# Two experts of the second layer loaded before the expert loop: the loop's block count is worked out from two items further on

## The chip, the cores and the metric

One core of a Trainium2 chip runs the whole program. The metric is the device time of one execution in microseconds (us), and the figure compared is the median over runs. TensorE is called PE, VectorE DVE, ScalarE ACT and GpSimd POOL; SP is the engine whose queue issues nearly all loads.

## What is computed

Two transformer layers over 256 latent tokens and 256 context tokens, width 1024, all in float32. The second layer returns the latents only, so its expert stage handles 256 tokens. What matters here is that stage:

```python
def moe(h, prm):
    t = h.reshape(B * N, D)
    scores = jax.nn.sigmoid((t @ prm["w_router"]).astype(jnp.float32))
    _, idx = lax.top_k(scores + prm["b_router"].astype(jnp.float32), TOP_K)      # 4 of 32 experts
    sel = jnp.take_along_axis(scores, idx, axis=-1)
    w = sel / jnp.sum(sel, axis=-1, keepdims=True) * ROUTED_SCALE
    ...
    gate = jnp.einsum("td,edf->tef", t, prm["w_gate_e"])      # 1024 x 256 for each expert
    up = jnp.einsum("td,edf->tef", t, prm["w_up_e"])          # 1024 x 256
    act = jax.nn.silu(gate) * up * comb[..., None]
    routed = jnp.einsum("tef,efd->td", act, prm["w_down_e"])  # 256 x 1024
```

Ahead of it in each layer stand the latents and attention (MLA), a short convolution, a Fourier mixing, 24 sigmoid gate groups that merge the three, and one output projection (`w_out`, 1024 x 1024).

## The kernel before

**Items.** The expert stage works in items. An item is one expert with up to `CAP[l]` of its tokens: 128 in the first layer, 64 in the second. Items 0 to 31 are experts 0 to 31. An expert with more tokens than `CAP[l]` gets a further item, and these follow as items 32, 33 and so on. DVE counts how many items hold tokens (`turns[0, 1]`, L2051 and after) and compares the count with `item_t[:, 4:8]`, which holds 32, 36, 40 and 44. The number of these four values that lie below the count is `more`.

**The loop.** Four items (`UNROLL`, u = 0 to 3) make a block. Block 0 stands ahead of the loop, written out; SP, POOL, ACT, PE and DVE then each run `Fori(1, more + BLOCKS)` with `BLOCKS` = 8. So 4 x (8 + `more`) items are run. An item behind the last one with tokens still loads weights (those of expert 0) and is computed; its column in the table of rows is the "absent" one, so it gathers and stores no row.

**An item's work.** SP loads 3 MiB of weights: gate and up, 1 MiB each, into `ring[u]` (`load_gate_up`, L656) and down, 1 MiB, into `dn[u]` (`load_down`, L671). A load into buffer u waits until PE has read the buffer for the item four earlier (`gu_full`, `y_full`). SP issues in order, so a load that waits holds back those behind it. POOL gathers the item's token rows from DRAM (L826) and stores its result rows (L838), half a row of 512 floats (2 KiB) to a partition in the second layer. PE transposes the rows (L1521), multiplies by gate and up (L1547: 8 chunks of the depth x 2 column halves, 256 columns each), transposes the activation (L1556) and multiplies by down (L1572). ACT and DVE take the results from PSUM.

**Ahead of the loop in the second layer.** SP walks through `stream`, a list in which each entry names its buffer (`slot`), who must have read the buffer before, and the source. `ukv` sits in slot 3, `uq` in slot 0, branch weights in the halves "0" and "0b", gate weights in slots 1 and 2 (slot 2 lies in `qkv`), and the two halves of `w_out` in slots 1 and 3, both loaded after the gates of the last branch. Then come gate/up of item 0 and down of items 0 and 1 (wait: last `y` group), after the output projection `tri`, the shared expert's weights into `ring[3]` (2 MiB), gate/up of items 1 and 2, down of items 2 and 3, and, once the shared expert has been multiplied (`sgu 1 1`), gate/up of item 3. The loop follows.

**The output projection.** For each half j of `w_out` and each of 8 chunks k, ACT makes a rounded copy (L1058) and DVE the remainder (L1951); PE (L1435 to L1437) multiplies with both, half j after half.

Of the kernel before, what the change touches and what calls it, by code (L numbers as in the profile page):

```python
# [16 lines left out]
P = 128  # L17
KC = DM // P
# [13 lines left out]
ROUNDS = 4  # L32
ADA_CHUNKS = 12
MAX_ITEMS = 48
# [145 lines left out]
def hybrid_layers(nc, I, C, out):  # L180
# [23 lines left out]
    with ctx:  # L204
# [64 lines left out]
        needed, over = part(1), part(4)  # L269
# [19 lines left out]
        h_hi = ring_lo[:, 2, :].rearrange("p (k t) -> p k t", k=KC)  # L289
# [23 lines left out]
        mT = qkv[:, 0:4096].rearrange("p (k t) -> p k t", k=KC)  # L313
# [10 lines left out]
        id_of = qkv[:, 688:704].rearrange("p (t k) -> p t k", k=TOPK)  # L324
        row_of_item = m_lo[:, 4:8, :].rearrange("p a b -> p (a b)").rearrange("p (n c) -> p n c", c=P)
# [15 lines left out]
        item_col, item_expert = tab[0:1, 136:136 + MAX_ITEMS], tab[0:1, 184:184 + MAX_ITEMS]  # L341
# [11 lines left out]
        gu = [ring[:, u, :].rearrange("p (a k n) -> p a k n", a=2, k=KC) for u in range(UNROLL)]  # L353
        gu_lo = [ring_lo[:, u, :].rearrange("p (a k n) -> p a k n", a=2, k=KC) for u in range(UNROLL)]
# [63 lines left out]
        gu_full = by_layer("gu_full")  # L418
        gu_part, e_hi_ready, e_lo_ready = one("gu_part"), one("e_hi_ready"), one("e_lo_ready")
# [58 lines left out]
        for l in range(DEPTH):  # L478
# [76 lines left out]
            for j, n in ((0, "1"), (1, "3")):  # L555
                item(n, ("psum", (l, "out", last, 1)), (l, "out", j), KC, at(I["w_out"][l], 512 * j, 512 * j + 512))
# [51 lines left out]
        def out_weights(l, j, k):  # L608

            n = stream[item_at[(l, "out", j)]][4]  # L610
            flat = lambda w: w[:, :, :, :].rearrange("p a k n -> p (a k n)")[:, 512 * (k % 4):512 * (k % 4) + 512]
            high = h_lo[:, k, :] if j else flat(w_hi if k < 4 else w_lo)
            return slot(l, "out", j)[:, k, :], high, area_lo[n][:, 512 * k:512 * k + 512]
# [14 lines left out]

        block = ctx.enter_context(nc.Block())

        @block.sync
        def _(sp):
# [15 lines left out]
            for l in range(DEPTH):  # L648
                act = ACTIVE[l]
                for n in range(first_item[l] + (3 if l else 0), first_item[l + 1]):  # L650
# [20 lines left out]
                def load_down(u, b, e, first=False):  # L671
                    if not first:
                        sp.wait_ge(y_full[l], 4 * b + u - 3)
# [6 lines left out]


                load_gate_up(0, 0, 0, first=True)
                for u in (0, 1):
                    load_down(u, 0, u, first=True)
# [4 lines left out]
                w = ring[:, SLOTS - 1, :].rearrange("p (a n) -> p a n", a=2)  # L689
                sp.dma_start(w[:, 0, :], by_p(I["w_gate_s"][l])).then_inc(shared_loaded, 16)  # L690
                sp.dma_start(w[:, 1, :], by_p(I["w_up_s"][l])).then_inc(shared_loaded, 16)
                load_gate_up(1, 0, 1, first=True)
                load_gate_up(2, 0, 2, first=True)
                for u in (2, 3):
                    load_down(u, 0, u, first=True)
                load_gate_up(3, 0, 3, first=True)
                wait_emptied(sp, l, "items")
                more = sp.value_load(more_u[0:1, 0:1], min_val=0, max_val=4)
                with nc.sync.Fori(1, more + BLOCKS) as b:
                    for u in range(UNROLL):  # L700
                        e = sp.value_load(item_expert[:, bass.ds(4 * b + u, 1)], min_val=0, max_val=NE - 1)
# [4 lines left out]
                if l == 0:  # L706
                    for n in range(first_item[1], first_item[1] + 3):
                        load_item(n)
                for u in range(UNROLL):
                    sp.wait_ge(y_stored[l][u], more * 16 + 16 * BLOCKS)  # L710
# [10 lines left out]
        def _(pool):  # L721
# [18 lines left out]
            for l in range(DEPTH):  # L740
# [34 lines left out]
                else:  # L775
                    pool.wait_ge(grow_stored, 48)
                    for n in range(2):
                        pool.dma_start(Grow[:, n, 0, :], grow_d[1][n:n + 1, :].to_broadcast([P, DM])).then_inc(grow_loaded, 16)

                for b in (1, 2):  # L780
                    for dc in range(KC):
                        n = (b - 1) * KC + dc
                        if l == 0 and n == 14:
                            load_cols(1)
                            pool.wait_ge(grow_stored, 32)
                            for s in range(2):
                                for m in range(2):
                                    pool.dma_start(Grow[:, m, s, :], grow_d[0][2 * s + m:2 * s + m + 1, :].to_broadcast([P, DM]))\
# [4 lines left out]
                        nc.gpsimd.tensor_tensor(mT[:, dc, 0:P * act], mT[:, dc, 0:P * act],  # L793
# [13 lines left out]

                def column(u, b):
                    return pool.value_load(item_col[:, bass.ds(4 * b + u, 1)], min_val=0, max_val=P)
# [7 lines left out]
                def gather(u, b, first=False):  # L817

                    n = u if first else column(u, b)
                    if not first:  # L820
                        pool.wait_ge(xt_full[l], 4 * b + u - 3)
# [3 lines left out]
                    copied((16 * b + 4 * u - 7) if not first else 2 * u + 1)  # L825
# [4 lines left out]
                def store(u, b, copies):  # L830

                    n = column(u, b)
                    pool.wait_ge(y_act[l], 4 * b + u + 1)
                    if l == 0:
# [5 lines left out]
                                            bounds_check=n_y, oob_is_err=False).then_inc(y_stored[l][u], 16)  # L840


                for u in range(UNROLL):
                    gather(u, 0, first=True)
                with nc.gpsimd.Fori(1, more + BLOCKS) as b:
                    for u in range(UNROLL):
                        gather(u, b)
                        store(u, b - 1, 16 * b + 4 * u - 5)
                for u in range(UNROLL):
                    store(u, more + (BLOCKS - 1), more * (4 * UNROLL) + (4 * NE - 7 + 2 * u))  # L850

        @block.scalar
        def _(act_e):
# [20 lines left out]
            for l in range(DEPTH):  # L874
# [49 lines left out]
                for k in range(KC):  # L924
                    nc.scalar.activation(h_hi[:, k, 0:n_tok], hT[:, k, 0:n_tok], ACT.Copy).then_inc(h_hi_ready[l], 1)
# [125 lines left out]
                for j in range(2):  # L1051
                    wait_arrived(act_e, l, "out", j)
                    for k in range(KC):
                        if j == 0:
                            act_e.wait_ge(merged[l], KC + k + 1)
                            nc.scalar.activation(h_hi[:, k, 0:n_tok], mT[:, k, 0:n_tok], ACT.Copy).then_inc(h_hi_ready[l], 1)
# [49 lines left out]

                def take_x(u, b, n=None):

                    act_e.wait_ge(xt_full[l], 4 * b + u + 1)
                    if n is None or n >= 2:  # L1110
                        act_e.wait_ge(gu_full[l], 4 * b + u - 1)
# [5 lines left out]
                def silus(u, b, n=None):  # L1117
                    act_e.wait_ge(gu_full[l], 4 * b + u + 1)
                    if n is None or n >= 2:
                        act_e.wait_ge(a_ready[l], 4 * b + u - 1)  # L1120
# [3 lines left out]
                def take_y(u, b, n=None):  # L1124

                    act_e.wait_ge(y_full[l], 4 * b + u + 1)
                    if n is None or n >= 2:

                        act_e.wait_ge(y_stored[l][(u - 2) % 4], 16 * b + (16 if u >= 2 else 0))
# [19 lines left out]
                else:  # L1149
                    for n in range(UNROLL):  # L1150
                        take_x(n, 0, n)
                        if n >= 1:
                            silus(n - 1, 0, n - 1)
                        if n >= 2:
                            take_y(n - 2, 0, n - 2)
# [37 lines left out]
        def _(pe):  # L1193
# [21 lines left out]
            for l in range(DEPTH):  # L1215
# [85 lines left out]
                for i, (name, f) in enumerate(IN_TILES):  # L1301
                    dst = group(l, name, f)
                    pe.wait_ge(w_lo_ready[l], i + 1)
                    for k in range(KC):
# [3 lines left out]
                        nc.tensor.matmul(dst[:, 0:n_tok], hi, h_hi[:, k, 0:n_tok], start=k == 0, stop=False)  # L1308
                        nc.tensor.matmul(dst[:, 0:n_tok], hi, h_lo[:, k, 0:n_tok], start=False, stop=False)  # L1309
                        ins = nc.tensor.matmul(dst[:, 0:n_tok], lo, h_hi[:, k, 0:n_tok], start=False, stop=k == KC - 1)  # L1310
# [89 lines left out]
                for b in range(3):  # L1400
                    for dc in range(KC):
# [5 lines left out]
                        for k in range(KC):  # L1407
                            hi, lo = w_hi[:, n % 2, k, :], gate_lo(l, n)[:, k, :]
                            nc.tensor.matmul(dst[:, 0:n_tok], hi, h_hi[:, k, 0:n_tok], start=k == 0, stop=False)  # L1409
                            nc.tensor.matmul(dst[:, 0:n_tok], hi, h_lo[:, k, 0:n_tok], start=False, stop=False)  # L1410
                            ins = nc.tensor.matmul(dst[:, 0:n_tok], lo, h_hi[:, k, 0:n_tok], start=False, stop=k == KC - 1)  # L1411
# [13 lines left out]
                for t in range(act):  # L1425
                    for j in range(2):
                        dst = group(l, "out", t, j)
                        for k in range(KC):
# [5 lines left out]
                            hi, lo = h_hi[:, k, tile(t)], m_lo[:, k, tile(t)]  # L1434
# [25 lines left out]
                def shared_in(f, a):  # L1460
# [3 lines left out]
                    w = gu[SLOTS - 1]  # L1464
# [20 lines left out]
                for n in range(act * TOPK):  # L1485
                    pe.wait_ge(id_ready, NTILE * TOPK * l + n + 1)
                    ins = nc.tensor.matmul(dst[:, 0:P], id_of_item[:, n, :], row_of_item[:, n, :], start=n == 0, stop=n == act * TOPK - 1)
# [24 lines left out]
                narrow = CAP[l] < P  # L1512

                def transpose_x(u, b, n=None):
                    pe.wait_ge(x_gathered[l][u], 16 * b + 16)
                    if n is None or n >= 1:
                        pe.wait_ge(xt_act[l], 4 * b + u)
                        pe.wait_ge(xt_dve[l], 4 * b + u)
# [5 lines left out]
                def gate_up(u, b):  # L1524
# [14 lines left out]
                    pe.wait_ge(gu_loaded[l][u], 32 * b + 32)  # L1539
                    pe.wait_ge(xt_act[l], 4 * b + u + 1)  # L1540
                    pe.wait_ge(xt_dve[l], 4 * b + u + 1)
                    x = xT[u % 2]
                    for k in range(KC):
                        xk = x[:, P * (k % 4) + 64 * (k // 4):P * (k % 4) + 64 * (k // 4) + 64]
                        for f in range(2):
                            w = gu[u][:, :, k, P * f:P * f + P]
# [4 lines left out]
                def transpose_a(u, b, n=None):  # L1551
                    pe.wait_ge(a_ready[l], 4 * b + u + 1)
                    if n is None or n >= 1:
                        pe.wait_ge(at_ready[l], 4 * b + u)
# [4 lines left out]
                def down(u, b, n=None):  # L1559
                    pe.wait_ge(at_ready[l], 4 * b + u + 1)  # L1560
                    pe.wait_ge(dn_loaded[l][u], 16 * b + 16)
                    if n is None or n >= 1:
                        pe.wait_ge(y_act[l], 4 * b + u)
                        if not narrow:
                            pe.wait_ge(y_dve[l], 4 * b + u)
                    for f in range(2):
                        for c in range(2):
                            if not narrow:
                                ins = nc.tensor.matmul(ps[:, 3072 + 512 * c:3584 + 512 * c], aT_e[u % 2][:, tile(f)],  # L1569
                                                       dn[u][:, f, 512 * c:512 * c + 512], start=f == 0, stop=f == 1)  # L1570
                            else:
                                ins = nc.tensor.matmul(ps[64 * c:64 * c + 64, 3072:3584], aT_e[u % 2][:, 64 * f:64 * f + 64],  # L1572
                                                       dn[u][:, f, 512 * c:512 * c + 512], start=f == 0, stop=f == 1,
# [3 lines left out]
                for n in range(UNROLL):  # L1577
# [681 lines left out]
```

## Time and profile before

| | us |
|---|---|
| median of 3 runs | 1688.69 |
| the runs | 1687.06 to 1694.16 |
| the profiled execution | 1688.29 |
| its span, first to last instruction | 1686.4 |

| | PE | DVE | ACT | POOL |
|---|---|---|---|---|
| busy, share of the span | 91% | 55% | 36% | 21% |

The profiled execution's time is 1.9 us more than its span. PE at 91% is an average over stages; the chain that ended last gives PE 69% of the span, DMA 14% and DVE 11%, and the line of DMA that stands out in it is the load of `in_w_up_e` with 10%. The mean granted clock of PE is 0.963 of 2.4 GHz. The second layer's expert loop is the last long stage, from 1366 us to 1645 us.

### The profile page before, as it was taken

What the parts mean: (1) busy time and instruction counts of PE and PEld (TensorE: products, weight loads), DVE (VectorE), ACT (ScalarE), POOL (GpSimd) and SP (SyncE); (2) the same over time, 40 slices, a digit from 0 to 9 for tenths busy, and PEclk for the clock granted to TensorE, in tenths of its full rate; (3) what the DMA queues carried; (4) which work ended last, traced back from release to release, by engine and by line L of the source; (5) the groups of instructions that cost most, each with busy time, mean ns of one, the idle gap of its engine ahead of it and who ended that gap; (6) DMA issues with size and microseconds to landing.
All of it is one profiled execution on the core that took longest, in us unless ns stands there. A gap on an engine that the chain in (4) does not pass through costs nothing.

```text
span 1686.4 us, 22672 instructions
## 1 busy us (share of the span) xinstructions
PE 1526.3 (91%) x7546; PEld 1064.8 (63%) x7546; DVE 919.8 (55%) x1579; ACT 599.8 (36%) x1034; POOL 352.8 (21%) x495
## 2 busy tenths in 40 slices
PE   5999999999988988999999987999999898888876
PEld 3677566677756755767767645866799664444442
DVE  1576778777885464777777734446656521110112
ACT  2332234423323433655656514334455511111111
POOL 3000000001112002465556520000011024333320
PEclk8999999999999989999999999999999999998998
DMA  9743340255566063899999973302255679999993
GB/s 334 255 155 123 125 150 1 76 200 189 185 239 230 31 252 128 294 369 359 364 371 367 354 249 119 124 29 100 88 188 191 252 264 414 415 414 415 416 372 138
DMA packets 122998, 393.88 MB, mean 234 GB/s; under 512 B 15556, under 2 KB 20116, under 8 KB 103472
## 3 DMA queue, kind: packets, MB, share of 16 engines
q1 hardware_dynamic: 104128, 359.42, 56.5%
q0 software_dynamic: 17440, 30.31, 5.2%
q10 hardware_dynamic: 1360, 3.23, 0.5%
q8 instruction: 43, 0.70, 0.2%
q14 instruction: 27, 0.22, 0.0%
HBM read 389.65 MB, written 30.50 MB: 249 GB/s over the span
## 4 chain that ended last, share of the span: by engine, by line
PE 69%; DMA 14%; DVE 11%; issue 2%; SPq 2%; ACT 1%; POOL 0%; POOLq 0%; DVEq 0%; ACTq 0%
PE ps L1212 14%; DMA ring<-in_w_up_e 10%; PE ps L1569 6%; PE ps L1547 3%; PE ps L1409 3%; PE ps L1532 3%; PE ps L1534 3%; PE ps L1533 3%; PE ps L1410 3%; PE ps L1411 3%; PE ps L1380 2%; DVE Grow L1712 2%; PE ps L1308 2%; PE ps L1309 2%; PE ps L1310 2%
## 5 line engine op out<-in xcount | busy, mean ns | idle before, releaser
L1547 PE MATMUL ps<-ring,oT_b 128*64 128x256 f32 x1152 | 154.2, 428 | 44.8 <-DMA ring<-in_w_up_e 44.2
L2073 DVE TENSOR_TENSOR ring_lo<-ring,m_lo 128x1024 fp32r<-128x1024 f32 x128 | 156.1, 1223 | 13.4 <-ACT m_lo L1094 4.0
L1547 PEld LDWEIGHTS ps<-ring,oT_b 128*64 128x64 f32 x1152 | 93.7, 153 | 96.9 <-DMA ring<-in_w_up_e 39.3
L1094 ACT ACTIVATE m_lo<-ring 128x1024 fp32r<-128x1024 f32 x128 | 135.5, 1061 | 42.3 <-PE ps L1534 31.9
L1409 PE MATMUL ps<-ring_lo,w_hi 128*128 128x512 f32 (+1 forms) x384 | 131.8, 343 | 3.9 <-DVE ring_lo L1899 3.7
L1712 DVE SCALAR_TENSOR_TENSOR Grow<-ring,small,Grow 128x512 f32<-128x512 f32 x182 | 131.1, 749 | 3.8
L2105 DVE TENSOR_TENSOR head<-ps,head 128x128 f32<-128x128 f32 (+1 forms) x68 | 23.9, 351 | 197.5 <-ACT head L1121 197.5
L1410 PE MATMUL ps<-h_lo,w_hi 128*128 128x512 f32 (+1 forms) x384 | 130.1, 339 | 0.0
L793 POOL TENSOR_TENSOR qkv<-qkv,head 128x512 f32<-128x512 f32 (+1 forms) x32 | 36.1, 1127 | 432.4 <-DVE head L1931 432.4
L838 POOL DMA_INDIRECT y_rows<-bT,small x68 | 99.3, 1460 | 27.2 <-issue 27.2
L1532 PE MATMUL ps<-m_lo,oT_lo 128*128 128x512 f32 x256 | 103.3, 404 | 0.0
L1533 PE MATMUL ps<-ring_lo,oT_lo 128*128 128x512 f32 x256 | 100.5, 392 | 0.0
L1534 PE MATMUL ps<-m_lo,h_lo 128*128 128x512 f32 x256 | 100.5, 392 | 0.0
L836 POOL COPY small<-wr 128x1 uint32 x68 | 34.4, 506 | 279.3 <-ACT bT L1130 148.3
L1308 PE MATMUL ps<-ring_lo,oT_lo 128*128 128x512 f32 (+1 forms) x256 | 87.1, 340 | 5.1 <-DVE ring_lo L1756 5.0
L1121 ACT ACTIVATE head<-ps 128x128 f32<-128x128 f32 (+1 forms) x68 | 21.8, 320 | 194.1 <-PE ps L1547 189.1
L1409 PEld LDWEIGHTS ps<-ring_lo,w_hi 128*128 128x128 f32 x384 | 73.6, 192 | 23.0 <-issue 14.1
L1309 PE MATMUL ps<-h_lo,oT_lo 128*128 128x512 f32 (+1 forms) x256 | 86.0, 336 | 0.0
L1035 ACT ACTIVATE tmp<-ps,small 128x512 f32<-128x512 f32 (+1 forms) x48 | 28.0, 583 | 160.6 <-PE ps L1411 160.0
L1410 PEld LDWEIGHTS ps<-h_lo,w_hi 128*128 128x128 f32 x384 | 73.7, 192 | 7.2
L1310 PE MATMUL ps<-ring_lo 128*128 128x512 f32 (+1 forms) x224 | 77.0, 344 | 0.0
L1212 PE MATMUL ps<-ring,hT 128*128 128x288 f32 (+1 forms) x224 | 64.3, 449 | 4.4 <-DVE hT L1741 4.4
(324 smaller groups left out, 3317.1 us busy)
## 6 DMA issues: line engine op xcount, KB each, us to landing
ring<-in_w_gate_e SPq DMA_DIRECT2D x68, 1024.0 KB, 9.5
ring<-in_w_up_e SPq DMA_DIRECT2D x68, 1024.0 KB, 13.8
ring<-in_w_ada SPq DMA_DIRECT2D x34, 1024.0 KB, 5.4
qkv<-in_w_down_e SPq DMA_DIRECT2D x34, 1024.0 KB, 14.6
ring<-in_w_in SPq DMA_DIRECT2D x13, 2048.0 KB, 10.1
cT<-in_w_down_e SPq DMA_DIRECT2D x17, 1024.0 KB, 9.4
fT<-in_w_down_e SPq DMA_DIRECT2D x17, 1024.0 KB, 11.0
qkv<-in_w_in SPq DMA_DIRECT2D x7, 2048.0 KB, 11.4
```

Of the source, the lines that this page charges most:

```text
L1094: nc.scalar.activation(pair(e_hi, j), pair(gu[u], j), ACT.Copy).then_inc(e_hi_ready, 1)
L1212: ins = nc.tensor.matmul(dst, a, b, start=n == 0, stop=n == len(pairs) - 1)
L1308: nc.tensor.matmul(dst[:, 0:n_tok], hi, h_hi[:, k, 0:n_tok], start=k == 0, stop=False)
L1309: nc.tensor.matmul(dst[:, 0:n_tok], hi, h_lo[:, k, 0:n_tok], start=False, stop=False)
L1409: nc.tensor.matmul(dst[:, 0:n_tok], hi, h_hi[:, k, 0:n_tok], start=k == 0, stop=False)
L1410: nc.tensor.matmul(dst[:, 0:n_tok], hi, h_lo[:, k, 0:n_tok], start=False, stop=False)
L1532: nc.tensor.matmul(ps[:, o:o + 512], hi, e_hi[:, :, k, :], start=k == 0, stop=False)
L1533: nc.tensor.matmul(ps[:, o:o + 512], hi, gu_lo[u][:, :, k, :], start=False, stop=False)
L1534: ins = nc.tensor.matmul(ps[:, o:o + 512], lo, e_hi[:, :, k, :], start=False, stop=k == KC - 1)
L1547: ins = nc.tensor.matmul(ps[64 * f:64 * f + 64, o:o + 256], xk, w, start=k == 0, stop=k == KC - 1, skip_group_check=True)
L1712: ins = V.scalar_tensor_tensor(into, w[:, k, :], by, into, ALU.mult, ALU.add)
L2073: V.tensor_tensor(pair(gu_lo[u], j), pair(gu[u], j), pair(e_hi, j).bitcast(f32), ALU.subtract).then_inc(e_lo_ready, 1)
```

## The change

In the second layer two experts are handled ahead of the four-item blocks (`AHEAD = [0, 2]`). Their 6 MiB of weights are loaded early into places that the second layer leaves half used, since it has 256 tokens where the first has 512:

- expert 0: gate and up into `ring[3]`, down into the context half of `xres`, issued behind `uq` and waiting for the last `kvup` group; behind it expert 1's gate into half of `ring[2]` and its up into half of `Grow`
- expert 1's down into half of the old `mT` area, issued behind the second gate item

Buffer u of block b now holds item 4b + u + 2. The written-out part has six items: two in buffers u = 2, 3 (block -1) and four of block 0. Item 1's gate and up lie apart, so PE multiplies them in two groups of 128 columns where all others take one of 256. The four thresholds for `more` become 34, 38, 42 and 46. The shared expert goes into `ring[1]`. Before the loop, gate/up of item 2 is loaded after the output projection, that of item 3 after the shared expert, that of item 5 after item 0's gate/up multiply and that of item 4 after item 1's. The second half of `w_out` goes into slot 0 in two halves, the later of them waiting for the last `y` group. The rest makes room: `mT`, `m_lo`, `h_hi`, the table of rows and the gate rows are packed closer in the second layer.

```diff
+AHEAD = [0, 2]
-MAX_ITEMS = 48
+MAX_ITEMS = 52
...
+        ahead_gate = ring[:, 2, 2048:4096].rearrange("p (k n) -> p k n", k=KC)
+        ahead_up = early_acc[:, 2048:4096].rearrange("p (k n) -> p k n", k=KC)
+        ahead_dn = [w.rearrange("p (k n) -> p k n", k=2) for w in
+                    (xres[:, 2:4, :].rearrange("p t d -> p (t d)"), qkv[:, 2048:4096])]
...
-            for j, n in ((0, "1"), (1, "3")):
-                item(n, ("psum", (l, "out", last, 1)), (l, "out", j), KC, at(I["w_out"][l], 512 * j, 512 * j + 512))
+            out_read = ("psum", (l, "out", last, 1))
+            item("1", out_read, (l, "out", 0), KC, at(I["w_out"][l], 0, 512))
+            if l == 0:
+                item("3", out_read, (l, "out", 1), KC, at(I["w_out"][l], 512, 1024))
+            else:
+                for i in range(2):
+                    item(("0", "0b")[i], out_read, (l, "out", 1, i), 4, at(I["w_out"][l][512 * i:512 * i + 512], 512, 1024), half=True)
...
+        prologue = lambda l: [(u, -1) for u in range(UNROLL - AHEAD[l], UNROLL)] + [(u, 0) for u in range(UNROLL)]
...
+                def load_ahead(i):
+
+                    by_k = lambda w: w[1, i].rearrange("(p k) n -> p k n", k=KC)
+                    if i == 0:
+                        wait_full(sp, 1, "kvup", NTILE - 1, 1)
+                    into = (gu[3][:, 0, :, :], gu[3][:, 1, :, :]) if i == 0 else (ahead_gate, ahead_up)
+                    sp.dma_start(into[0], by_k(I["w_gate_e"])).then_inc(ahead_loaded[i], 16)
+                    sp.dma_start(into[1], by_k(I["w_up_e"])).then_inc(ahead_loaded[i], 16)
...
+                    if l and stream[n][0] == (l, "uq"):
+                        load_ahead(0)
+                        load_ahead_down(0)
+                        load_ahead(1)
+                    if l and stream[n][0] == (l, "gate", 0, 1):
+                        load_ahead_down(1)
...
-                        sp.wait_ge(gu_full[l], 4 * b + u - 3)
+                        sp.wait_ge(gu_full[l], 4 * b + (u - 3 + off))
+                    elif l:
+                        if u == 1:
+                            wait_full(sp, l, "sgu", 1, 1)
+                        elif u >= 2:
+                            sp.wait_ge(gu_full[l], 4 - u)
...
+                    load_gate_up(0, 0, 2, first=True)
+                    for u in (2, 3):
+                        load_down(u, 0, u + off, first=True)
+                    load_gate_up(1, 0, 3, first=True)
+                    load_gate_up(3, 0, 5, first=True)
+                    load_gate_up(2, 0, 4, first=True)
...
+                    if early == 1:
+                        for a, w in enumerate((ahead_gate, ahead_up)):
+                            for k in range(KC):
+                                xk = x[:, P * (k % 4) + 64 * (k // 4):P * (k % 4) + 64 * (k // 4) + 64]
+                                for f in range(2):
+                                    ins = nc.tensor.matmul(ps[64 * f:64 * f + 64, o + P * a:o + P * a + P], xk, w[:, k, P * f:P * f + P],
+                                                           start=k == 0, stop=k == KC - 1, skip_group_check=True)
...
-                for n in range(UNROLL):
-                    transpose_x(n, 0, n)
+                seq = prologue(l)
+                for n in range(len(seq)):
+                    transpose_x(*seq[n], n)
...
-                link(V.tensor_scalar(over[0:1, :], item_t[0:1, 4:8], turns[0:1, 1:2], None, ALU.is_lt))
+                link(V.tensor_scalar(over[0:1, :], item_t[0:1, 4:8], float(AHEAD[l]), turns[0:1, 1:2], ALU.add, ALU.is_lt))
```

## Rows read from the trace of the kernel before

**Rows 1.** Windows in layer 2: us, busy us (instructions), PEclk, DMA share, GB/s

```profile
1102.00:1140.00 38.00, 36.28 (x173) 24.69 (x173) 12.47 (x24) 10.98 (x26) 0.00 (x0) 1.00 0.09 32
1140.00:1196.00 56.00, 52.11 (x255) 34.41 (x254) 39.34 (x104) 24.45 (x56) 0.00 (x0) 1.00 0.20 75
1196.00:1217.00 21.00, 19.13 (x147) 19.08 (x147) 11.52 (x18) 10.53 (x17) 0.00 (x0) 0.92 0.29 101
...
1373.00:1379.40 6.40, 6.28 (x47) 3.39 (x47) 1.27 (x4) 0.94 (x3) 0.00 (x0) 1.00 0.89 328
...
1391.00:1417.00 26.00, 25.27 (x187) 14.34 (x185) 3.72 (x13) 5.42 (x14) 12.01 (x25) 1.00 1.02 414
1417.00:1645.00 228.00, 184.18 (x1212) 102.05 (x1211) 24.89 (x82) 32.53 (x82) 74.46 (x159) 0.91 1.00 406
```

**Rows 2.** Waits from 1366 us to 1660 us: who for whom, us, times, longest

```profile
PE ps L1547 <- DMA ring<-in_w_up_e: 44.2, 28, 2.9
```

**Rows 3.** SP's queue in order of time: start us, us, line, what is loaded

```profile
1303.79 0.34 SPq L668 DMA_DIRECT2D ring<-in_w_gate_e  x1
...
1366.27 0.34 SPq L668 DMA_DIRECT2D ring<-in_w_gate_e  x1
...
1373.20 0.35 SPq L668 DMA_DIRECT2D ring<-in_w_gate_e  x1
...
1380.73 0.34 SPq L668 DMA_DIRECT2D ring<-in_w_gate_e  x1
```

**Rows 4.** Issue to landing of the up loads issued at 1373.66 and 1622.14

```profile
DMA to landing us min/median/max: 8.9/8.9/8.9
...
DMA to landing us min/median/max: 23.1/23.1/23.1
```

**Rows 5.** The last two stores of result rows, in POOL's timeline

```profile
1654.46 1.01 POOL L838 DMA_INDIRECT y_rows<-bT,small  x1 [0.54 <-issue]
...
1657.35 1.00 POOL L838 DMA_INDIRECT y_rows<-bT,small  x1 [0.80 <-issue]
```

**Rows 6.** POOL's DMA queue, windows 1654.5:1657.3 and 1657.3:1659.6: packets, MB, share

```profile
q0 software_dynamic: 80, 0.02, 3.1%
...
q0 software_dynamic: 80, 0.00, 1.7%
```

**Rows 7.** The chain that ended last, its last stage: start us, us, what

```profile
1374.04 3.60 PE ps L1547 x32
1377.64 1.72 PE ps L1572 x8
...
1613.28 0.23 issue
...
1622.14 23.06 DMA ring<-in_w_up_e
1645.19 0.23 issue
1645.42 5.36 PE ps L1547 x32
```

**Rows 8.** PE's weight loads of one item's gate and up, in the timeline

```profile
1369.33 3.22 PEld L1547 LDWEIGHTS ps<-ring,oT_b 128*64 128x64 f32 x32 [0.17 <-issue]
```

**Rows 9.** PE's timeline: the `kvup` groups, and the first gate group

```profile
1118.05 13.97 PE L1212 MATMUL ps<-ring,qkv 128*128 128x512 f32 x32 [0.94 <-ACT oT_b L956]
...
1197.95 0.36 PE L1409 MATMUL ps<-ring_lo,w_hi 128*128 128x256 f32 x1 [1.87 <-DVE ring_lo L1899]
```

**Rows 10.** Splitting `w_out` in ACT's and DVE's timeline, second half last

```profile
1309.35 4.27 ACT L1058 ACTIVATE h_lo<-ring 128x512 fp32r<-128x512 f32 x8
...
1312.17 4.89 DVE L1951 TENSOR_TENSOR ring_lo<-ring,h_lo 128x512 fp32r<-128x512 f32 x8
```

**Rows 11.** Issue to landing of gate at 1303.79 and the second down load

```profile
DMA to landing us min/median/max: 4.8/4.8/4.8
...
DMA to landing us min/median/max: 11.0/11.0/11.0
```

More of the change, by code:

```diff
@@ L268, in hybrid_layers @@
         sel = item_t[:, 8:10]
-        needed, over = part(1), part(4)
+        needed = part(1)
         half_id = part(1)
@@ L418, in hybrid_layers @@
         gu_full = by_layer("gu_full")
+        ahead_loaded = [one(f"ahead_loaded_{i}") for i in range(2)]
+        ahead_stored = [one(f"ahead_stored_{i}") for i in range(2)]
         gu_part, e_hi_ready, e_lo_ready = one("gu_part"), one("e_hi_ready"), one("e_lo_ready")
@@ L708, in _ @@
                         load_item(n)
+                all_stored = more * 16 + 16 * BLOCKS
                 for u in range(UNROLL):
-                    sp.wait_ge(y_stored[l][u], more * 16 + 16 * BLOCKS)
+                    sp.wait_ge(y_stored[l][u], all_stored)
+                for i in range(off):
+                    sp.wait_ge(ahead_stored[i], 16)
                 for t in range(act):
@@ L828, in gather, with store @@
                                             bounds_check=n_g, oob_is_err=False).then_inc(x_gathered[l][u], 16)
-                def store(u, b, copies):
-                    n = column(u, b)
-                    pool.wait_ge(y_act[l], 4 * b + u + 1)
+                def store(u, b, copies, first=None):
+                    n = column(u, b) if first is None else first
+                    pool.wait_ge(y_act[l], 4 * b + (u + 1 + off))
                     if l == 0:
@@ L839, in store @@
                                             in_=y_e[u % 2][:, 0:wide[l]], in_offset=None,
-                                            bounds_check=n_y, oob_is_err=False).then_inc(y_stored[l][u], 16)
-                for u in range(UNROLL):
-                    gather(u, 0, first=True)
+                                            bounds_check=n_y, oob_is_err=False)\
+                        .then_inc(ahead_stored[first] if l and first is not None and first < off else y_stored[l][u], 16)
+                seq = prologue(l)
+                for n, (u, b) in enumerate(seq):
+                    gather(u, b, first=n)
+                    if n >= UNROLL:
+                        store(*seq[n - UNROLL], 16 * b + (4 * u - 5 + 4 * off), first=n - UNROLL)
                 with nc.gpsimd.Fori(1, more + BLOCKS) as b:
@@ L847, in _ @@
                         gather(u, b)
-                        store(u, b - 1, 16 * b + 4 * u - 5)
+                        store(u, b - 1, 16 * b + (4 * u - 5 + 4 * off))
                 for u in range(UNROLL):
-                    store(u, more + (BLOCKS - 1), more * (4 * UNROLL) + (4 * NE - 7 + 2 * u))
+                    store(u, more + (BLOCKS - 1), more * (4 * UNROLL) + (4 * NE - 7 + 2 * u + 4 * off))
         @block.scalar
@@ L1600, in _ @@
                     if t == act - 1:
-                        pe.wait_ge(y_act[l], more * UNROLL + NE)
+                        pe.wait_ge(y_act[l], more * UNROLL + (NE + off))
                         if not narrow:
```

201 lines of the change are left out of this document (119 added, 82 removed).

## The prediction

> **What bounds the kernel now.** I read the shares of busy time first and trusted them least: PE at 91% is an average. Then the windows of the second layer [rows 1]. Up to 1217 us DMA is nearly idle (share 0.09, 0.20, 0.29). From 1391 to 1417 us it is full at 414 GB/s, and from 1417 to 1645 us full at 406 GB/s, while DVE and ACT work a tenth of the time. The waits say the same: in the expert loop PE waited for the up load 28 times, 44.2 us in all [rows 2]. The chain of waits closes it: for each block of four items it goes once through "DMA ring<-in_w_up_e", 23.06 us for the last one, then PE [rows 7]. So from about 1373 us on the time is set by how many MiB are still to be moved, and by nothing that an engine does.
>
> One load checks this. The up load of item 4 is issued at 1373.66 and lands 8.9 later, at 1382.6; that of item 35, issued at 1622.14, lands 23.1 later, at 1645.2 [rows 4]. Between them lie 31 items of 3 MiB, so 93 MiB in 262.6 us, 2.82 us for a MiB with the rows that POOL gathers and stores in between. Bare, a MiB (1.049 MB) at 414 GB/s takes 2.53 us. The last block, whose items hold few rows, took from 1613.28 to 1645.19, 31.9 us for 12 MiB, 2.66 us each [rows 7].
>
> **How many items will run.** This is the step on which all hangs. The change saves only if `more` becomes 0, which needs at most 34 items with tokens. The profile of before tells how many there are. Item 34, the 35th, is stored by the second to last store, issued at 1654.46, and item 35 by the last, issued at 1657.35 [rows 5]. POOL's DMA queue moved 0.02 MB for the former and 0.00 MB for the latter, with as many packets [rows 6]. An absent row moves nothing, and a token's result is two halves of 2 KiB, so 0.02 MB are about five tokens. The 35th item holds tokens, the 36th none: `turns` is 35. Before, 35 lies above 32 and not above 36: `more` is 1 and 36 items run. After, 35 lies above 34 and not above 38: `more` is again 1, and 2 + 4 x 9 = 38 items run, not 34. Items 35, 36 and 37 are empty and load 3 MiB each all the same.
>
> **The sum, in MiB.** Count what is still to be loaded once the shared expert is done, at 1366.27 [rows 3]. Before: 36 x 3 less gate/up of items 0 to 2 (6) and four down loads (4), so 98. After: 38 x 3 less the 6 ahead, gate/up of item 2 (2) and four down loads (4), so 102. Two experts came out of the loop's traffic, two empty ones went in, and one ring buffer less is filled beforehand, since `ring[1]` holds the shared expert, `ring[3]` expert 0 and half of `ring[2]` expert 1. The difference is +4 MiB. Bounds: 4 x 2.53 = 10.1 us if they carry no rows at all, 4 x 2.82 = 11.3 us at the loop's mean. I take the last block's 2.66, since the added items are empty like most of that block: +10.6 us.
>
> The Trainium skill (DMA: Bandwidth & Descriptors, Specifications) gives a limit of about 358 GB/s for one core's reads from HBM. The rows do not bear it out here, at 414 GB/s. By that rule, as an estimate, the 4 MiB would cost 11.7 us.
>
> **The start of the loop, where DMA could fall idle.** Before, SP issues item 3's gate/up at 1366.27, item 4's at 1373.20 when item 0's multiply ends, item 5's at 1380.73 [rows 3]. After, the same two places carry items 3 and 5; item 4's follows item 1's multiply, which ends at 1374.04 + 3.60 = 1377.6 [rows 7], earlier than the 1380.73 of before. Item 6's follows item 2's multiply, about 6 us later, while DMA is still busy with item 4's. Before left DMA about 0.1 idle from 1373 to 1379.4 [rows 1], under 1 us. So the new order costs nothing, or gives back up to 0.7.
>
> Against it stands item 1's multiply in groups of 128 columns: as many columns, twice as many weight loads. Not in the trace; the bounds are 0 (the columns' 3.60 us stays) and +3.6 (32 loads show 3.22 us busy [rows 8], and 64 would take 6.4 and more). All later issues slip by it, and DMA has about 2 us of queued work against that. I take 0 of cost, with 1.6 at the worst end.
>
> The Trainium skill (TensorE: Matmul & The Clock Gate, Back-to-back issue gap) says that a stream of pairs of weight load and 128-column matmul sustains some 81 ns each, where one alone takes 56. As an estimate, 64 of them are 5.2 us, 1.6 more than the row's 3.60. That would stay under the 2 us, so the sum would not move; no row here shows it.
>
> **What is hidden, and by what.** The first 5 MiB ahead wait for the last `kvup` group, which is multiplied from 1118.05 and done at about 1132 [rows 9]. At 414 GB/s they take 12.7 us, to about 1147. Behind them in SP's queue stand the first branch and gate weights, which PE needs only with the first gate group at 1197.95 [rows 9]: over 40 us of cover. The sixth MiB goes at 1196 behind a gate load, with DMA at 0.29 [rows 1]; 2.5 us. Without that cover each MiB would cost 2.5 us. These loads also take nothing off the path before 1366: DMA is not what the router and the shared expert wait for.
>
> The later half of `w_out`'s second half now waits for the last `y` group, so it goes where item 0's gate load went, at 1303.79 [rows 3], and that one landed in 4.8 us, at 1308.6 [rows 11]. ACT begins that half of `w_out` at 1309.35 and spends 4.27 on 8 chunks, so the fifth comes at 1311.5; DVE starts at 1312.17 [rows 10]. 2.9 us of slack, cost 0. At the other end, if it shares the engines with the two down loads behind it and lands as late as the second of those (11.0 [rows 11], 1314.8), ACT stalls for 3.3 us, and PE with it. Added waits at the end of SP's program (`ahead_stored`) are met long before. POOL's written-out part is as long as before with its stores 4 behind. The rest is renaming. From the last up landing at 1645.2 to the end of the span 41 us stay as they are, but for PE's clock: item 35's multiply took 5.36 us where others took 3.60 [rows 7], after a wait in a stretch whose granted clock is 0.91 on the mean [rows 1]; this can fall the other way by 1.7.
>
> **Sum.** 1688.3 (the profiled execution) + 10.6 = 1698.9 us. The median of before, 1688.69, stands 0.4 from it. That is +0.6%.
>
> **Rivals.**
> - *It does as it says: 34 items.* It decides at whether the 35th item holds tokens. Then 34 x 3 - 12 = 90 MiB remain instead of 98, and 8 MiB less are 8 x 2.66 = 21.2 us: 1667. For it: only the stated number. Against it: the 0.02 MB of item 34's store [rows 6]. Chance 0.06.
> - *38 items, but the extra is partly given back.* Bare rate (10.1), the 0.7 of idle DMA gone, the last multiply as fast as the others (1.7): +7.7, 1696.0, inside 0.5%. Chance 0.22.
> - *38 items and the covers fail.* `w_out` lands late (+3.3) and item 1's multiply at double time idles DMA (+1.6): +15.5, 1703.8. Chance 0.12.
> - *Forecast*: 0.60, about 1697 to 1702.
>
> Some 0.5% (8.4 us) is what a measurement can tell from no change. The forecast and the third rival lie above it: slower 0.72. The second rival: same 0.21. The first, and a remainder of other gains: faster 0.07. The range of 8 in 10 takes the forecast, most of the second rival and the lower edge of the third, 1694.5 to 1704.
>
> **What would show it.** 38 gate loads, 38 stores and a last store with 0.00 MB in the second layer; three of the last four items without rows. Up loads from the one landing near 1382.6 to the last: 97 MiB in about 273 us. The first loads ahead at about 1132, DMA share up in that window and no new wait of PE before 1300. ACT's fifth chunk of `w_out` without a wait. The end of the span 41 us behind the last up landing. Wrong would be: 34 stores in the second layer, a loop shorter by 21 us, or a stall of PE in the output projection.

## The result

The changed kernel takes 1701.1 us (median of 4 runs, 1699.6 to 1703.0), the kernel before, beside it, 1689.6 us (1687.1 to 1694.2). The ratio is 1.0062, with an interval of 95% from 1.0045 to 1.0079: slower by 10.5 us, 7.6 to 13.3. (The two medians lie 11.5 us apart; the ratio is estimated from all the runs and not from the medians. For the experiments below the distance of the medians is given beside the ratio.) The forecast was 1698.9 in a range of 1694.5 to 1704. A second comparison on other runs gave 1.0063 (1.0045 to 1.0081), with medians of 1702.1 and 1690.7. All these runs are fast ones. 38 items ran, not 34.

The page of the profile after: the span, then the busy shares, then SP's DMA queue (packets, MB, share).

```profile
span 1699.6 us, 22982 instructions
...
PE 1538.9 (91%) x7668; PEld 1072.7 (63%) x7668; DVE 922.1 (54%) x1585; ACT 602.9 (35%) x1040; POOL 358.5 (21%) x507
...
q1 hardware_dynamic: 105264, 365.71, 56.9%
```

Busy shares tell nothing: PE is at 91% in both. The bytes of SP's queue do: 365.71 MB. The same line of before:

```profile
q1 hardware_dynamic: 104128, 359.42, 56.5%
```

That is 6.3 MB or 6 MiB more, just two more items of 3 MiB.

### The profile page after: what moved, and what is told of

It reads as the page before. It is cut to its first block, busy times and chain, and to the rows that moved or that the text cites. A ratio compares the mean times of both kernels' runs of the same rounds, so it can differ in the third digit from the quotient of the medians.

```text
span 1699.6 us, 22982 instructions
## 1 busy us (share of the span) xinstructions
PE 1538.9 (91%) x7668; PEld 1072.7 (63%) x7668; DVE 922.1 (54%) x1585; ACT 602.9 (35%) x1040; POOL 358.5 (21%) x507
## 3 DMA queue, kind: packets, MB, share of 16 engines
q1 hardware_dynamic: 105264, 365.71, 56.9%
## 4 chain that ended last, share of the span: by engine, by line
PE 71%; DMA 14%; DVE 10%; issue 2%; SPq 2%; ACT 1%; POOL 0%; DVEq 0%; POOLq 0%; ACTq 0%
PE ps L1287 14%; DMA ring<-in_w_up_e 10%; PE ps L1663 6%; PE ps L1635 4%; PE ps L1608 3%; PE ps L1610 3%; PE ps L1609 3%; PE ps L1484 3%; PE ps L1486 3%; PE ps L1485 3%; PE ps L1455 2%; DVE Grow L1807 2%; PE ps L1383 2%; PE ps L1597 2%; PE ps L1384 2%
## 5 line engine op out<-in xcount | busy, mean ns | idle before, releaser
L1635 PE MATMUL ps<-ring,oT_b 128*64 128x256 f32 x1184 | 157.9, 427 | 43.9 <-DMA ring<-in_w_up_e 43.9
L1163 ACT ACTIVATE m_lo<-ring 128x1024 fp32r<-128x1024 f32 x128 | 135.5, 1061 | 42.2 <-PE ps L1610 31.9
L901 POOL COPY small<-wr 128x1 uint32 (+1 forms) x70 | 34.7, 496 | 281.1 <-ACT bT L1204 150.9
L1184 ACT ACTIVATE oT_lo<-ps 128x1024 fp32r<-128x1024 f32 x32 | 32.8, 1026 | 98.7 <-issue 69.0
## 6 DMA issues: line engine op xcount, KB each, us to landing
qkv<-in_w_down_e SPq DMA_DIRECT2D x35, 1024.0 KB, 10.4
ring<-in_w_in SPq DMA_DIRECT2D x13, 2048.0 KB, 10.1
```

The costliest lines, as they stand in the source:

```text
L1163: nc.scalar.activation(pair(e_hi, j), pair(gu[u], j), ACT.Copy).then_inc(e_hi_ready, 1)
L1635: ins = nc.tensor.matmul(ps[64 * f:64 * f + 64, o:o + 256], xk, w, start=k == 0, stop=k == KC - 1, skip_group_check=True)
```

## The profile after, beside the rows of before

**How many items ran.** The DMA issues in the window of the second layer's expert stage, first of the kernel before, then of the changed one (the count behind x is that of the stores, one for each item):

```profile
y_rows<-bT,small POOLq DMA_INDIRECT x36, 6.6
```

```profile
y_rows<-bT,small POOLq DMA_INDIRECT x38, 6.6
```

POOL's timeline of the changed kernel, its last four stores, items 34 to 37:

```profile
1654.05 1.03 POOL L903 DMA_INDIRECT y_rows<-bT,small  x1 [0.55 <-issue]
1659.94 1.02 POOL L903 DMA_INDIRECT y_rows<-bT,small  x1 [0.51 <-issue]
1668.08 1.01 POOL L903 DMA_INDIRECT y_rows<-bT,small  x1 [0.42 <-issue]
1671.13 1.01 POOL L903 DMA_INDIRECT y_rows<-bT,small  x1 [0.85 <-issue]
```

And POOL's DMA queue in the window behind each of them (packets, MB, share), in the same order:

```profile
q0 software_dynamic: 79, 0.02, 1.5%
...
q0 software_dynamic: 80, 0.00, 0.6%
...
q0 software_dynamic: 80, 0.00, 1.3%
...
q0 software_dynamic: 80, 0.00, 1.7%
```

Item 34 carries 0.02 MB, as before [rows 6]; items 35, 36 and 37 carry nothing. Each of the three still had 3 MiB of weights loaded for it.

**The loop.** The chain of waits of the changed kernel, its last stage:

```profile
1372.27 5.31 PE ps L1635 x32
...
1378.60 3.64 PE ps L1627 x64
1382.24 1.72 PE ps L1666 x8
...
1629.01 0.23 issue
...
1637.65 22.96 DMA ring<-in_w_up_e
1660.61 0.23 issue
1660.84 3.67 PE ps L1635 x32
```

It has the shape of before [rows 7]: through the up load once a block, and 31.6 us from 1629.01 to 1660.61 for the last block, where before took 31.9. The last landing has moved from 1645.2 to 1660.6, 15.4 us. The span grew by 13.2. To split that, take SP's queue of the changed kernel:

```profile
1105.56 0.39 SPq L671 DMA_DIRECT2D ring<-in_w_uq  x1
1134.98 0.34 SPq L683 DMA_DIRECT2D ring<-in_w_gate_e  x1
...
1306.72 0.37 SPq L671 DMA_DIRECT2D ring<-in_w_out  x1
...
1369.05 0.34 SPq L719 DMA_DIRECT2D ring<-in_w_gate_e  x1
...
1377.60 0.33 SPq L719 DMA_DIRECT2D ring<-in_w_gate_e  x1
...
1382.28 0.33 SPq L719 DMA_DIRECT2D ring<-in_w_gate_e  x1
```

The kernel before issues `uq` at

```profile
1102.62 0.39 SPq L646 DMA_DIRECT2D ring<-in_w_uq  x1
```

- Up to `uq`, ahead of anything that the change alters in the order of the loads, the changed kernel is already 2.9 us late. From `uq` to the first load after the shared expert it takes 263.5 us, before 263.7 [rows 3]. The 2.9 us lie ahead of `uq` and vary: over nine profiles (those of the experiments below included) `uq` goes out between 1102.6 and 1111.7. Three profiles of the old structure have 1102.6, 1104.9 and 1108.2, mean 1105.2; six of the new one have 1105.6 to 1111.7, mean 1107.8. With that scatter an offset of the change ahead of `uq` is neither shown nor excluded.
- From that load to the last up landing: 291.6 us where before took 278.9, +12.6 (1369.05 to 1660.61, and 1366.27 to 1645.19).
- From the last landing to the end: 39.0 us where before took 41.2, -2.2. Of these 1.7 are item 35's 5.36 us, now 3.67 for item 37; the rest are the last read of result rows and the last multiply of the span, 0.4 and 0.4, with small steps against them.

The windows of the last item's gate/up multiply, before and after, in the columns of [rows 1]. The third number from the end is PE's granted clock as a share of 2.4 GHz:

```profile
1645.40:1650.80 5.40, 5.38 (x34) 3.98 (x36) 0.00 (x0) 0.00 (x0) 0.38 (x1) 0.68 0.18 71
...
1660.80:1664.50 3.70, 3.66 (x34) 2.98 (x36) 0.00 (x0) 0.00 (x0) 0.17 (x1) 1.00 0.19 73
```

The same multiply ran at a mean of 0.68, between 1.2 and 2.4 GHz, before, and at 2.4 GHz after. This repeats: 5.36 us in all three profiles of the old structure (and in that of three items ahead, below), 3.67 in all five of the structure with two items ahead.

**The start of the loop and the hidden parts.** Windows of the changed kernel: us, busy us (instructions) of PE, PEld, DVE, ACT and POOL, then PE's clock, DMA share, GB/s.

```profile
1102.00:1140.00 38.00, 36.09 (x185) 25.41 (x185) 14.51 (x28) 12.04 (x27) 0.00 (x0) 1.00 0.20 70
1140.00:1196.00 56.00, 52.11 (x249) 34.53 (x247) 39.34 (x104) 21.78 (x52) 0.00 (x0) 1.00 0.37 143
...
1352.00:1366.00 14.00, 12.72 (x62) 10.42 (x62) 7.80 (x31) 2.05 (x3) 1.85 (x5) 1.00 0.07 23
1366.00:1373.00 7.00, 5.03 (x29) 3.73 (x29) 1.27 (x3) 0.77 (x2) 4.82 (x10) 0.98 0.49 162
1373.00:1379.40 6.40, 6.28 (x49) 3.83 (x47) 0.98 (x3) 0.66 (x2) 0.53 (x1) 0.76 0.69 261
...
1417.00:1656.00 239.00, 197.47 (x1317) 109.60 (x1315) 26.50 (x87) 35.46 (x87) 80.88 (x171) 0.91 1.01 411
```

The early MiB show as DMA share 0.20 and 0.37 where before had 0.09 and 0.20 [rows 1], and PE is as busy as before in 1140 to 1196, 52.11 us. From 1373 to 1379.4 DMA stands at 0.69 where before had 0.89. Item 0's multiply took 5.31 us, at a granted clock of 0.68 from 1372.2 to 1377.6, and SP can issue item 5's load only behind it, at 1377.60, 8.6 us behind the one ahead of it. Before it, from 1369.0 to 1372.3, PE had stood idle for 1.36 and 0.61 us around a short group of transposes.

It looks as if 1.7 us of the +12.6 were the clock at this one place. The second profile of the same kernel says no. There the pauses are 1.27 and 0.60 us, the clock stays at 1.00, the multiply takes 3.63 and the distance is 6.8 us, and still the stretch from the first load to the last up landing is 291.9 us. The first 41 us of that stretch, in the kernel before, the changed one and its second profile:

```profile
1366.27:1407.27 41.00, 38.85 (x298) 22.22 (x300) 6.82 (x21) 7.51 (x19) 16.50 (x36) 1.00 0.95 366
...
1369.05:1410.05 41.00, 38.94 (x316) 23.09 (x318) 6.82 (x21) 7.64 (x19) 15.26 (x34) 0.96 0.89 346
...
1370.72:1411.72 41.00, 39.03 (x332) 23.52 (x334) 6.82 (x21) 7.63 (x19) 16.45 (x36) 1.00 0.94 357
```

At 406 GB/s the bytes missing against before are worth 2.0 us in the first profile and 0.9 in the second. In the rest of the stretch DMA moves 406 GB/s before and in the first profile, and 404 in the second, which is another 1.2 us. So a loss of about 2 us repeats, but not at one place, and its cause stays open.

**The output projection.** Waits of PE from 1303 to 1335, after:

```profile
PE ps L1510 <- DVE ring_lo L2046: 2.1, 1, 2.1
```

Before has the same single wait of 2.1 us there. ACT's second half of `w_out`, after:

```profile
1312.28 4.27 ACT L1127 ACTIVATE h_lo<-ring 128x512 fp32r<-128x512 f32 x8
```

Eight chunks in 4.27 us, exactly as before [rows 10]. The last quarter of `w_out`, issued at 1306.72, landed in 5.2 us, at 1311.9; ACT's fifth chunk comes at 1314.4, so it was there 2.5 us ahead.

## The experiments

The theory: the end is set by how many MiB are still to be moved once the shared expert is done, at 2.5 to 2.7 us each. The rival: empty items are nearly free, and the other parts of the change (split multiply, moved `w_out`, early loads, order of the first loads) cost the 10.5 us. Each run is given against the kernel before on the same chip.

**Fewer items by other data.** One expert's bias is lowered, so that 34 items hold tokens.

```diff
+                if l:
+                    link(V.tensor_scalar(biased[:, 0:act, 9:10], biased[:, 0:act, 9:10], -0.05, None, ALU.add))
                 for t in range(act):
                     link(V.max(m8[:, t, :], biased[:, t, :]))
```

> The changed kernel, with 0.05 taken off the router's bias of expert 9 in the second layer. That expert then has about 50 tokens instead of 76 and the items with tokens should fall from 35 to 34, so the block count drops by one; the output differs from the reference for the tokens that change expert. Theory A (the time goes by the MiB still to be moved after the shared expert): 90 MiB where the kernel before has 98, so 8 x 2.66 = 21 us less than before, about 1668 us, and 12 MiB or 32 us less than the changed kernel. Theory B (empty items are cheap, and the 11.5 us of the change come from its other parts: the split multiply, the moved half of w_out, the later start of the loop): at most a few us less than the changed kernel, 1695 us or more. 34 stores of result rows in the second layer under both.

Measured: 0.9874 (0.9853 to 0.9896), 1670.9 us against 1691.5. The stores of the stage:

```profile
y_rows<-bT,small POOLq DMA_INDIRECT x34, 6.4
```

That is 20.6 us less than before and, adding the two comparisons, 31 to 32 us less than the changed kernel. The same code but for the two added lines, with the count of items on the other side of a threshold, goes from slower to clearly faster. The rival's other parts are all still in it. At the price of the next two experiments, 2.48 and 2.52 us a MiB, the 8 MiB less come to 19.8 to 20.2 us, so those other parts together cost nothing that shows. Of the 8 MiB, 6 belong to the two items that do not run; only 2 are room gained, since 12 MiB are loaded before the shared expert is done where before had 10.

The same data on the kernel before, with the same two lines added:

> The kernel before with the same 0.05 taken off expert 9's bias; the output differs from the reference for the tokens that change expert. 34 is still above 32, so 36 items run, two of them empty. Theory A and B: within 1 us of the kernel before. Were it faster by several us, the rows moved and not the weights would set the loop's time, and the first run of this call would have to be read against this one.

Measured: 1.0009 (0.9994 to 1.0024), 1693.2 us against 1691.5. The medians lie 1.7 us apart, a little over the expected 1 us, but the interval includes no change. The data by themselves change nothing that can be measured.

**More items in the kernel before.**

```diff
-                link(V.tensor_scalar(over[0:1, :], item_t[0:1, 4:8], turns[0:1, 1:2], None, ALU.is_lt))
+                link(V.tensor_scalar(over[0:1, :], item_t[0:1, 4:8], -4.0 * l, turns[0:1, 1:2], ALU.add, ALU.is_lt))
```

> The kernel before with its thresholds in the second layer lowered by 4, so that one more block runs: 40 items, 5 of them empty. Theory A: 12 MiB more, 12 x 2.53 to 12 x 2.66 = 30 to 32 us more than before, about 1720 us. Theory B: an empty block costs what its multiplies cost at most, 4 x 6.0 = 24 us if PE set the pace, and near 0 if it is hidden.

Measured: 1.0176 (1.0154 to 1.0198), 1721.3 us, +29.7 for four empty items, 2.48 us a MiB and just under the 30 to 32 expected. Its waits for the up load, where before had 44.2 us in 28 waits [rows 2]:

```profile
PE ps L1547 <- DMA ring<-in_w_up_e: 51.0, 29, 2.8
```

An empty item costs 7.4 us. PE's instructions need 6.0 us for an item, as the start of the loop in the kernel before shows, where the multiplies follow each other without a wait for weights (1374.04, 1380.05 and 1386.08, by the chain of waits). So the item costs more than its computation; that the rest is its bytes is for the next experiment to show.

**Fewer bytes, the same items.** In the changed kernel's loop only half of each down load is made.

```diff
-                    sp.dma_start(dn[u], I["w_down_e"][l][bass.ds(e, 1)].rearrange("a (k p) n -> p (a k) n", p=P))\
-                        .then_inc(dn_loaded[l][u], 16)
+                    src = I["w_down_e"][l][bass.ds(e, 1)].rearrange("a (k p) n -> p (a k) n", p=P)
+                    if l and not first:
+                        sp.dma_start(dn[u][:, 0:1, :], src[:, 0:1, :]).then_inc(dn_loaded[l][u], 16)
+                    else:
+                        sp.dma_start(dn[u], src).then_inc(dn_loaded[l][u], 16)
```

> The changed kernel with the down loads inside the second layer's loop cut to the first of their two halves (the second half keeps the block before's weights; the output differs from the reference). The same 38 items and the same number of DMAs, 32 x 0.5 = 16 MiB less. Theory A (bytes): 16 x 2.53 to 16 x 2.66 = 40 to 43 us less than the changed kernel, unless PE's 6.0 us an item gets in the way, which it should not (38 items leave DMA at 7.0 us an item). A rival, that a fixed cost of an item or of a DMA sets the pace and not its bytes: under 5 us less.

Measured: 0.982 (0.98 to 0.9841), 1661.8 us, where the changed kernel beside it took 1702.1. 40.3 us less for 16 MiB, 2.52 us each. Same items, same count of DMAs: it is the bytes. A window in the middle of this kernel's loop:

```profile
1400.00:1600.00 200.00, 178.05 (x1311) 100.51 (x1309) 26.45 (x87) 35.59 (x87) 83.13 (x175) 0.99 1.02 411
```

DMA is still full at 411 GB/s, with PE close behind at 178 of 200 us.

**Is loading early worth anything?** The six MiB are issued after the output projection instead.

```diff
-                    if l and stream[n][0] == (l, "uq"):
-                        load_ahead(0)
-                        load_ahead_down(0)
-                        load_ahead(1)
-                    if l and stream[n][0] == (l, "gate", 0, 1):
-                        load_ahead_down(1)
...
+                if l:
+                    load_ahead(0)
+                    load_ahead_down(0)
+                    load_ahead(1)
+                    load_ahead_down(1)
                 if l == 0:
                     load_gate_up(1, 0, 1, first=True)
```

> The changed kernel with the six early MiB issued only after the output projection, behind the shared expert's weights, instead of during latents and gates. Theory A as in the prediction: what is loaded after the shared expert stays 102 MiB, but 6 MiB more have to pass between 1333 and 1366 us, where 7 MiB (shared 2, item 2's gate and up 2, two down loads 2, and 1 of token rows) passed before. DMA stood at 0.07 from 1352 to 1366, so 5 to 6 MiB fit there: 0 to 4 us more than the changed kernel. If each MiB loaded early were worth its 2.66 us, it would be 16 us more.

Measured: 1.0074 (1.0053 to 1.0095), 1704.0 us against 1702.1 for the changed kernel: +1.9, with runs that overlap (1701.2 to 1706.0 and 1698.9 to 1705.3). Its windows before the loop:

```profile
1352.00:1359.00 7.00, 6.35 (x33) 5.34 (x34) 6.55 (x26) 0.00 (x0) 0.00 (x0) 0.56 1.01 373
1359.00:1366.00 7.00, 7.00 (x40) 5.96 (x39) 3.94 (x19) 1.67 (x2) 0.00 (x0) 0.95 1.01 424
1366.00:1373.00 7.00, 6.79 (x32) 5.64 (x30) 0.27 (x2) 0.38 (x1) 4.09 (x9) 1.00 0.68 262
```

The loads fill the stretch that stood at 0.07 in the changed kernel. The last load behind them, the down load issued at about 1345, lands at 1371 to 1372, just ahead of the first load after the shared expert at 1372.82. From `uq` to that load this kernel takes 263.9 us, 0.4 more than the changed one, while the other kernels spread from 262.5 to 263.9. From there to the last up landing it takes 291.5 us, as in the changed kernel's profiles. What counts is that the MiB are in place when the loop begins. That they are loaded during attention brings about 2 us by the medians, and with runs that overlap that much nothing is shown.

**All 35 items and no more.** A third item stands ahead of the blocks, so that 3 + 32 = 35 run. Its weights go into `ring[0]` and the last down buffer after the output projection, and the blocks take the ring's parts in the order in which they fall free. The rest follows from `off = 3`.

```diff
-AHEAD = [0, 2]
+AHEAD = [0, 3]
...
+        gu_late = [gu[1], gu[3], gu[2], gu[0]]
...
-                    load_gate_up(0, 0, 2, first=True)
-                    for u in (2, 3):
-                        load_down(u, 0, u + off, first=True)
-                    load_gate_up(1, 0, 3, first=True)
-                    load_gate_up(3, 0, 5, first=True)
-                    load_gate_up(2, 0, 4, first=True)
+                    by_k = lambda w: w[1, 2].rearrange("(p k) n -> p k n", k=KC)
+                    sp.dma_start(gu[0][:, 0, :, :], by_k(I["w_gate_e"])).then_inc(ahead_loaded[2], 16)
+                    sp.dma_start(gu[0][:, 1, :, :], by_k(I["w_up_e"])).then_inc(ahead_loaded[2], 16)
+                    load_down(2, 0, 5, first=True)
+                    load_ahead_down(2)
+                    load_gate_up(0, 0, 3, first=True)
+                    load_gate_up(1, 0, 4, first=True)
+                    load_gate_up(2, 0, 5, first=True)
+                    load_gate_up(3, 0, 6, first=True)
+                    load_down(3, 0, 6, first=True)
```

> The changed kernel with three items ahead of the blocks instead of two, so that 3 + 4 x 8 = 35 items run, each of them with tokens. The third one's weights are not loaded early: gate and up go into ring[0] and down into the last down buffer after the output projection, as item 2's do now; the ring buffers of the blocks are taken in the order in which they come free. Theory A: 105 - 6 - 2 - 4 = 93 MiB after the shared expert where before has 98, 5 x 2.66 = 13 us less than before, about 1676 us. Theory B: no better than the changed kernel by more than 5 us, about 1696 us or more.

Measured: 0.9932 (0.9905 to 0.9959), 1680.4 us against 1691.5: faster than both kernels, by 11.2 us than the one before (13 were expected) and, adding the comparisons, some 22 us than the changed one.

```profile
y_rows<-bT,small POOLq DMA_INDIRECT x35, 6.9
```

**All of them on one line.** From SP's first load after the shared expert to the end of the span, which leaves out the first layer's scatter. The MiB are counted as in the prediction.

| kernel | items | MiB left | first load, us | span, us | between, us | to the last up landing | behind it |
|---|---|---|---|---|---|---|---|
| changed, half down loads | 38 | 86 | 1369.67 | 1661.9 | 292.2 | 252.8 | 39.5 |
| changed, other data | 34 | 90 | 1375.56 | 1674.9 | 299.3 | 259.7 | 39.6 |
| 3 ahead | 35 | 93 | 1370.53 | 1677.2 | 306.7 | 265.7 | 41.0 |
| before | 36 | 98 | 1366.27 | 1686.4 | 320.1 | 278.9 | 41.2 |
| before, other data | 36 | 98 | 1370.69 | 1690.7 | 320.0 | 279.1 | 41.0 |
| changed | 38 | 102 | 1369.05 | 1699.6 | 330.6 | 291.6 | 39.0 |
| changed, second profile | 38 | 102 | 1370.72 | 1703.3 | 332.6 | 291.9 | 40.6 |
| changed, loads late | 38 | 102 | 1372.82 | 1703.5 | 330.7 | 291.5 | 39.2 |
| before, one block more | 40 | 110 | 1368.39 | 1719.1 | 350.7 | 310.0 | 40.8 |

From 90 to 110 MiB it is 51.4 us for 20 MiB, 2.57 us each. No difference shows between 34 and 35 items with tokens, nor from when the early weights were loaded. What was not varied is the traffic of the token rows, which goes through POOL's queue, 8.1 to 8.2 MB in every profile of this stretch: 2.57 us is the price of a MiB of weights on top of it. The kernel with half down loads lies some 3 us above the line; PE is close behind DMA there.

The last two columns split the distance and show what the sum hides. Within one structure the price is even: 12 MiB cost 31.9 us from 90 to 102 in the changed kernel (2.66 each), and 31.0 from 98 to 110 in the old one (2.58 each). But from the old structure (98) to the changed one (102) the 4 MiB come with 12.4 to 13.0 us, about 2 more than at that price. Behind the last landing the changed kernel gives 0.3 to 2.2 us back, as its last multiply takes 3.67 us and not 5.36. The two differences oppose each other, and the column "between" lies on one line.

## Why the prediction was right

- **The bound and the count of items** were right. `turns` is 35, read from the 0.02 MB of one store. The profile after shows 38 items, three of them empty, and the run with 34 shows the other branch at -20.6 us, where the first rival said -21.2.
- **+4 MiB at 2.66 us** was right in mechanism and in price: 2.66 and 2.58 us within either structure, 2.48 and 2.52 by the medians of the experiments. (In its count the text speaks of one ring buffer less; the +4 MiB are two, as only item 2's gate and up go there ahead of time where before items 0 to 2 did. The sum is right.)
- **That the total came so close is in part luck.** The stretch to the last up landing grew by 12.4 to 13.0 us in three profiles against two, outside the sum's own bounds of 10.1 to 11.3; the tail shrank by 0.3 to 2.2 us. What was off by 2 us one way and by up to 2 us the other gave +10.4 to +12.6 us between the first load and the end.
- **The start of the loop "costs nothing, or gives back up to 0.7"** was not borne out. A loss of about 2 us repeats in all three profiles. The row of DMA at 0.69 shows part of it in the first one only, and no run shows its cause.
- **Item 1's split multiply at 0** was right: 64 records in 3.64 us, where an unsplit one takes 3.60, so 57 ns each. The Trainium skill's sustained 81 ns for pairs of weight load and 128-column matmul (TensorE: Matmul & The Clock Gate, Back-to-back issue gap) does not hold for these weights of 64 columns; the row is at the lone matmul's 56. The estimate of 1.6 us more did not come about.
- **`w_out` at 0** was right, without a new wait: 2.5 us of slack where 2.9 were worked out.
- **The limit of 358 GB/s** (the Trainium skill, DMA: Bandwidth & Descriptors, Specifications) is passed again: 411 GB/s over 239 us, with one core running the program.
- **"Without that cover each MiB would cost 2.5 us"** was wrong. The late loads had no such cover and cost 0.3 us each by the medians, and nothing by the distances within the profiles. I had seen only the first idle stretch of DMA as cover; the second one, 1352 to 1366, right ahead of the loop, takes 6 MiB as well. The cover itself was there: the first five loads ahead go out at 1134.98 and the last of them lands at about 1151. (1132 and 12.7 us give 1145 and not the 1147 of the text, and the loads took 16 us; against over 40 us neither matters.)
- **The tail** of 41 us came out at 39.0, 40.6 and 39.2. The 1.7 us of the last multiply's clock, which the second rival counted in, were gained each time; why PE is granted 2.4 GHz there after the change was not tested; what PE did before it differs, as told at the end. The rest is the last multiply of the span, 8.7 to 10.1 us long in the three profiles.

## What to carry to other kernels

Before crediting a change with work it removes, find the number that decides it in the trace: here a threshold on a count that depends on the data, read from the bytes of the last stores. Where a loop runs in blocks, a shift of its start must be matched to the count of items, or padding eats the gain: 3 ahead were faster, 2 ahead slower. In a stage bound by DMA, count the MiB left at its start; here loading ahead paid by the room that it found, and no more for being early. And when a forecast comes true, compare its terms too: here two of them were off and made up for each other.

## What was not expected of the hardware

- 6 MiB more between the output projection and the loop, with DMA full from 1338 to 1366 at 373 to 424 GB/s, left the router's and the shared expert's chain as it was: 263.9 us, where eight other profiles have 262.5 to 263.9.
- Code with the same first layer reaches `uq` at times 6 us apart from profile to profile (1102.6 to 1108.2 in the old structure, 1105.6 to 1111.7 in the new one), more than half of the effect looked for. Only distances within one profile could tell the parts apart.
- The same last multiply of an item was granted 0.68 of 2.4 GHz in each of the three profiles of the old structure and in that of 3 items ahead, and at full 2.4 GHz in all five with 2 ahead. In the kernel before PE had waited 1.7 us for the up load ahead of the last but one multiply and 2.3 us ahead of the last; in the changed kernel 0 and 2.4 us.
